# Last block of a three-block network: the order of remainders, residual additions, turns of x and ScalarE's work around the output projection and the query projection

## The reference, cut to what matters

```python
def second_block(x, mem, positions, ...):
    h = rmsnorm_2(x, norm_mix_g)
    x = x + parallel_mixer(h, ...)            # mLSTM heads and causal attention, then @ w_out
    h = rmsnorm_2(x, norm_x_g)
    mem_n = rmsnorm_2(mem, norm_mem_g)
    x = x + memory_cross_attention(h, mem_n, wq_x, wkv_x, xq_norm_g, xk_norm_g, wo_x)
    h = rmsnorm_2(x, norm_ffn_g)
    x = x + jnp.square(jax.nn.relu(h @ w_ff1)) @ w_ff2
    return x

def memory_cross_attention(h, mem_n, wq_x, wkv_x, xq_norm_g, xk_norm_g, wo_x):
    q = rmsnorm_2((h @ wq_x).reshape(Bn, S, 4, 128), xq_norm_g)
    k, v = ...                                # mem_n @ wkv_x, k normed with xk_norm_g
    s = jnp.einsum('bshd,bnhd->bhsn', q, k) * 128 ** -0.5
    o = jnp.einsum('bshn,bnhd->bshd', jax.nn.softmax(s), v)
    return o @ wo_x
```

## Time and profile before

| | |
|---|---|
| three runs | 1669.36, 1673.74, 1679.61 us, median 1673.74 |
| profiled execution | 1671.81 us, span 1670.0 us |
| busy in the span | TensorE 1321.4 us (79%), VectorE 574.6 (34%), ScalarE 369.8 (22%), GpSimd 28.0 (2%) |
| chain that ended last | TensorE 43%, DMA 42%, VectorE 8%, ScalarE 3% |
| granted TensorE clock, mean | 0.908 of full |

### The profile page before, as it was taken

How to read it: one execution, slowest core, us unless ns; L and a number is a source line. 1 busy time by engine, 2 the same in 40 slices (tenths; PEclk the granted TensorE clock), 3 DMA queues, 4 the chain that set the end, 5 groups by cost and what they waited for, 6 DMA issues and landing times.

```text
span 1670.0 us, 30118 instructions
## 1 busy us (share of the span) xinstructions
PE 1321.4 (79%) x12602; PEld 898.3 (54%) x12602; DVE 574.6 (34%) x1202; ACT 369.8 (22%) x642; POOL 28.0 (2%) x54
## 2 busy tenths in 40 slices
PE   4899998765666666789877666666668998889999
PEld 2798584432223223389744322322225887779997
DVE  2575663111001001047531101001013677765555
ACT  2412532000000000054400000000003335544443
POOL 3020100000000000000000000000000000000000
PEclk8999999989888788799999878889788999999999
DMA  9988799999999999995799999999999630455540
GB/s 341 357 279 303 256 403 390 398 422 422 422 422 422 422 421 422 416 361 170 265 420 410 422 422 422 421 422 422 422 422 390 210 130 27 127 177 187 192 151 26
DMA packets 145936, 548.40 MB, mean 328 GB/s; under 512 B 9742, under 2 KB 77744, under 8 KB 96840
## 3 DMA queue, kind: packets, MB, share of 16 engines
q1 hardware_dynamic: 143216, 542.97, 82.9%
q10 hardware_dynamic: 1080, 3.64, 0.6%
q0 software_dynamic: 1568, 0.77, 0.4%
HBM read 546.29 MB, written 1.05 MB: 328 GB/s over the span
## 4 chain that ended last, share of the span: by engine, by line
PE 43%; DMA 42%; DVE 8%; ACT 3%; issue 2%; SPq 1%; DVEq 0%; ACTq 0%
DMA ring<-in_moe_w_up 33%; PE bank L766 8%; DMA ring<-in_moe_w_down 7%; PE bank L880 5%; PE bank L607 5%; PE bank L1302 5%; PE bank L567 3%; PE bank L903 2%; PE bank L630 2%; PE bank L661 2%; DMA ring<-in_attn_w_in 1%; DMA ring<-in_ada_w 1%; DVE ring_split L1620 1%; PE bank L781 1%; SPq L2686 1%
## 5 line engine op out<-in xcount | busy, mean ns | idle before, releaser
L880 PE MATMUL bank<-ring,scratch 128*32 128x256 f32 x3840 | 295.8, 456 | 151.5 <-DMA ring<-in_moe_w_up 102.5
L880 PEld LDWEIGHTS bank<-ring,scratch 128*32 128x32 f32 x3840 | 131.1, 127 | 302.6 <-DMA ring<-in_moe_w_up 158.2
L903 PE MATMUL bank<-ring,scratch 128*32 128x256 f32 x1984 | 153.1, 453 | 60.6 <-DMA ring<-in_moe_w_down 45.5
L1576 DVE COPY scratch<-bank 128x256 f32<-128x256 f32 x32 | 13.6, 425 | 430.0 <-PE bank L889 430.0
L766 PE MATMUL bank<-scratch_split,ring_split 128*128 128x256 f32 x1248 | 151.2, 283 | 3.7 <-DVE ring_split L1620 3.7
L766 PEld LDWEIGHTS bank<-scratch_split,ring_split 128*128 128x128 f32 x1248 | 150.3, 191 | 5.3 <-DVE ring_split L1620 4.1
L903 PEld LDWEIGHTS bank<-ring,scratch 128*32 128x32 f32 x1984 | 64.6, 127 | 142.3 <-DMA ring<-in_moe_w_down 76.4
L1620 DVE TENSOR_TENSOR ring_split<-ring,ring_split 128x2048 fp32r<-128x2048 f32 x48 | 110.0, 2292 | 74.2 <-ACT ring_split L2270 74.0
L2257 ACT ACTIVATE scratch<-bank 128x256 f32<-128x256 f32 x32 | 12.3, 384 | 484.9 <-PE bank L880 484.9
L2270 ACT CAST ring_split<-ring 128x2048 fp32r<-128x2048 f32 x48 | 91.5, 1907 | 59.8 <-PE bank L1302 36.7
L1583 DVE TENSOR_TENSOR scratch<-bank,moe_gate 128x256 f32<-128x256 f32 x32 | 13.6, 425 | 241.0 <-PE bank L903 241.0
(11 more groups left out here) (462 smaller groups left out, 1584.5 us busy)
## 6 DMA issues: line engine op xcount, KB each, us to landing
ring<-in_moe_w_down SPq DMA_DIRECT2D x124, 1024.0 KB, 26.4
ring<-in_moe_w_gate SPq DMA_DIRECT2D x120, 1024.0 KB, 25.1
ring<-in_moe_w_up SPq DMA_DIRECT2D x120, 1024.0 KB, 26.6
ring<-in_ada_w SPq DMA_DIRECT2D x48, 1024.0 KB, 9.2
ring<-in_w_ff SPq DMA_DIRECT2D x32, 1024.0 KB, 5.4
ring<-in_conv_w_in SPq DMA_DIRECT2D x12, 1024.0 KB, 12.4
ring<-in_attn_w_in SPq DMA_DIRECT2D x10, 1024.0 KB, 11.5
ring<-in_w_in SPq DMA_DIRECT2D x7, 1024.0 KB, 12.0
```

The costliest lines, as they stand in the source:

```text
L880: mm = nc.tensor.matmul(GU[32 * j:32 * j + 32, m * 256:(m + 1) * 256], xs[:, k % 2, 16 * k - k % 2 * 16:16 * k - k % 2 * 16 + 32], W[k % 2 ...
L903: mm = nc.tensor.matmul(Y[32 * g:32 * g + 32, 0:256], actT[:, b, 32 * j:32 * j + 32], W[b][:, g * 256:(g + 1) * 256], start=(j + b == 0), ...
```

## The change

On TensorE: the keys are turned ahead of out2.0; n3.3 is turned within qx.0's first pass, behind the first two quarters; the query heads are turned in two goes, each behind the evacuation of its unit, and the scores wait for the second tile only at the fifth; n4.0 to n4.2 go to banks 4 to 6 and n4.3 to bank 7, within ff1.0's first pass behind the first two quarters; the accumulators are claimed at ff2.0 and not ahead of ff1.0. On VectorE: the remainder of ff1.0's weights stands behind the second addition of ox, that of ff1.1's behind the third, and the row remainders behind all four. On ScalarE: in the causal attention the evacuation of out2m.0 and the rounding of out2.0's weights stand behind the last copy of probabilities and not ahead of it; n3.1 and n3.2 are rounded ahead of the last squares; the roots of the query heads and the load of the exponential's table stand between the two tiles of heads.

```diff
@@ -536,9 +536,9 @@
 
             return slice(256 * (k // 2) + k % 2, 256 * (k // 2) + 256, 2)
 
-        def pe_turn_rows(pe, name, src, n=KD, paired=False):
-
-            for b in range(n // 2):
+        def pe_turn_rows(pe, name, src, n=KD, paired=False, tiles=None):
+
+            for b in tiles or range(n // 2):
                 T = tile(pe, f"{name}.{b}")
                 for i in range(4):
                     k, t = 2 * b + i // 2, i % 2
@@ -546,9 +546,9 @@
                     mm = nc.tensor.transpose(T[:, i * P:(i + 1) * P], src[:, t, cols], ident)
                 done(f"{name}.{b}", mm)
 
-        def pe_turn_part(pe, name, u):
-
-            T = tile(pe, f"{name}.{u}")
+        def pe_turn_part(pe, name, u, bank=None):
+
+            T = tile(pe, f"{name}.{u}", bank=bank)
             for i in range(4):
                 k = 2 * u + i // 2
                 mm = nc.tensor.transpose(T[:, i * P:(i + 1) * P], x[:, i % 2, k * P:(k + 1) * P], ident)
@@ -610,7 +610,8 @@
             in0_read[u] = (full[place[name][0]], place[name][1])
             release[seat[("in0", u)]] = in0_read[u]
 
-        def pe_late(pe, n, name, h, rows=None, ts=range(TT), bank=None):
+        def pe_late(pe, n, name, h, rows=None, ts=range(TT), bank=None, last_turn=None):
+
 
 
             key, k0, kk = LATE[n]
@@ -623,6 +624,8 @@
             whole_bank = len(ts) == TT
             for i, (ht, wt) in enumerate(((h[0], hi), (h[0], lo), (h[1], hi))):
                 for k2 in range(0, kk, 2):
+                    if last_turn is not None and i == 0 and k2 == kk // 2:
+                        last_turn()
                     if rows and i != 1:
                         sig(rows[i // 2]).take(pe)
                     for t in ts:
@@ -742,6 +745,9 @@
 
             sig("w_hi").take(pe, (1, len(CONV_ORDER))[p])
             for b in range(4):
+                if p == 1 and b == 2:
+                    sig("x_ready").take(pe)
+                    pe_turn_part(pe, "n4", 3, bank=7)
                 sig(("h1_hi", "h4_hi")[p]).take(pe)
                 run(hi, h[0], (2 * b, 2 * b + 1), first=True)
             pe_split_unit(pe, p, 0)
@@ -1255,27 +1261,33 @@
                 pe_late(pe, u, f"out2m.{u}", (hm_hi, hm_lo))
             sig("oa_ready").take(pe)
             pe_turn_rows(pe, "oaT", oa, 4)
+            sig("kx_ready").take(pe)
+            pe_turn_rows(pe, "kxT", kx, 4)
             for u in range(4):
                 pe_late(pe, 4 + u, f"out2.{u}", (oa_hi, oa_lo), ("oa_hi", "oa_lo") if u == 0 else None)
-                if u == 1:
-                    sig("kx_ready").take(pe)
-                    pe_turn_rows(pe, "kxT", kx, 4)
                 if u >= 1:
                     sig("x_ready").take(pe)
                     pe_turn_part(pe, "n3", u - 1)
-            sig("x_ready").take(pe)
-            pe_turn_part(pe, "n3", 3)
+
+            def turn_last():
+                sig("x_ready").take(pe)
+                pe_turn_part(pe, "n3", 3)
+
+            pe_late(pe, 8, "qx.0", (h3_hi, h3_lo), ("h3_hi", "h3_lo"), last_turn=turn_last)
+            pe_late(pe, 9, "qx.1", (h3_hi, h3_lo))
             for u in range(2):
-                pe_late(pe, 8 + u, f"qx.{u}", (h3_hi, h3_lo), ("h3_hi", "h3_lo") if u == 0 else None)
-            copied(pe, "qx.0")
-            copied(pe, "qx.1")
-            pe_turn_rows(pe, "qxT", qx, 4)
-            for n in ("kxT.0", "kxT.1", "qxT.0", "qxT.1"):
+                copied(pe, f"qx.{u}")
+                pe_turn_rows(pe, "qxT", qx, 4, tiles=(u,))
+            for n in ("kxT.0", "kxT.1", "qxT.0"):
                 copied(pe, n)
-            pe_attend(pe, "c", 8, lambda i: 2,
-                      lambda T, i: nc.tensor.matmul(T[:, 0:SEQ], qxT[:, i // 2, (i % 2) * P:(i % 2 + 1) * P],
-                                                    kxT[:, i // 2, :], start=True, stop=True),
-                      lambda i, b: vx[:, b, (i // 2) * P:(i // 2 + 1) * P])
+
+            def score_c(T, i):
+                if i == 4:
+                    copied(pe, "qxT.1")
+                return nc.tensor.matmul(T[:, 0:SEQ], qxT[:, i // 2, (i % 2) * P:(i % 2 + 1) * P],
+                                        kxT[:, i // 2, :], start=True, stop=True)
+
+            pe_attend(pe, "c", 8, lambda i: 2, score_c, lambda i, b: vx[:, b, (i // 2) * P:(i // 2 + 1) * P])
             for i in range(8):
                 copied(pe, f"co{i}")
             pe_turn_rows(pe, "oxT", ox, 4)
@@ -1283,14 +1295,13 @@
                 pe_late(pe, 10 + u, f"ox.{u}", (ox_hi, ox_lo), ("ox_hi", "ox_lo") if u == 0 else None)
                 if u >= 1:
                     sig("x_ready").take(pe)
-                    pe_turn_part(pe, "n4", u - 1)
-            sig("x_ready").take(pe)
-            pe_turn_part(pe, "n4", 3)
-            acc = [tile(pe, f"ff2.{i}", bank=4 + i) for i in range(4)]
+                    pe_turn_part(pe, "n4", u - 1, bank=3 + u)
             for n, (name, u) in enumerate(FF_ORDER):
                 if name == "ff1":
                     pe_turned_split(pe, 1, n, f"ff1.{u}", (h_hi, h_lo), bank=u % 4)
                 else:
+                    if u == 0:
+                        acc = [tile(pe, f"ff2.{i}", bank=4 + i) for i in range(4)]
                     sig("w_split").take(pe)
                     release[seat[(name, u)]] = (sig("w_split").sem, sig("w_split").taken[pe.engine])
                     hi, lo = (z[n % 2].rearrange("p (a n) -> p a n", a=2) for z in w_parts[1])
@@ -2129,14 +2140,9 @@
                     empty(v, f"n4.{b}", ins)
                     give("h4_split", V.tensor_copy(st[:, 249:250], ident[:, 0:1]))
 
-            rest_of_weights(1, 0)
-
-            def beside_ox():
-                rest_of_weights(1, 1)
-                rest_of_rows((0, 1))
-
-            residual("ox", 4, None, "x_ready", beside=beside_ox)
-            rest_of_rows((2, 3))
+            residual("ox", 4, None, "x_ready", between=lambda: rest_of_weights(1, 0),
+                     beside=lambda: rest_of_weights(1, 1))
+            rest_of_rows(range(4))
             sig("squares_ready").take(v)
             step(V.tensor_reduce(rs4, pieces[:, :, 0:4], AX, ALU.add))
             step(V.tensor_scalar(rs4, rs4, 1.0 / D, EPS, ALU.mult, ALU.add))
@@ -2557,7 +2563,7 @@
                             load_table(ACT.Exp)
                         if i == 6:
                             round_late(8)
-                        if i == 7:
+                        if i == 8:
                             part_out("out2m", 0, part2)
                             round_late(4)
 
@@ -2575,17 +2581,19 @@
             load_table(ACT.Sqrt)
             for i in range(4):
                 if i >= 2:
-                    rounded("n3", "h3_hi", h3_hi, plain("norm_x_g_2"), (i - 2,))
+                    rounded("n3", "h3_hi", h3_hi, plain("norm_x_g_2"), (0,) if i == 2 else (1, 2))
                 sig("x_ready").take(s)
                 ins = piece_squares((i,), 256)
             sig("squares_ready").give(ins)
-            rounded("n3", "h3_hi", h3_hi, plain("norm_x_g_2"), (2, 3))
+            rounded("n3", "h3_hi", h3_hi, plain("norm_x_g_2"), (3,))
             round_late(9)
             roots(rs3, 2)
             round_late(10)
             round_late(11)
-            turned("qxT", qxT, lambda k: (vcol("xq_norm_g_2"), None), (0, 1))
+            turned("qxT", qxT, lambda k: (vcol("xq_norm_g_2"), None), (0,))
             roots(qn, 8)
+            load_table(ACT.Exp)
+            turned("qxT", qxT, lambda k: (vcol("xq_norm_g_2"), None), (1,))
             attend("c")
             round_late(12)
             for b in range(2):
```

## The result

| | before | after |
|---|---|---|
| 20 runs each, median | 1673.62 us (1665.34 to 1679.61) | 1665.20 us (1657.71 to 1671.21) |
| profiled execution, span | 1670.0 us | 1663.4 us |

The ratio is 0.995 with a 95% interval of 0.9937 to 0.9963: the change takes 6 to 10.5 us off, 8.4 in the medians, where 7.3 were forecast. Both programs scatter by some 14 us from run to run, so the interval is wide beside the effect, and what the single steps did is read from the traces.

What follows compares the result with a forecast made beforehand. TensorE was taken as the bound of the feed-forward loop; 6.1 us at the output projection and ff1.0 plus 1.2 upstream made 7.3, so 1671.8 became 1664.5, or 1666.5 us as a median, range 1660.5 to 1673.5.

Steps and rivals of the forecast that it cites:

- The bound and the place of the gain: TensorE bounds the feed-forward loop from 1492.61 us, so moving ff1.0's end moves the kernel's end one for one.
- Output projection and ff1.0: From ox.0 to ff1.0's end: VectorE's additions go first, TensorE's waits shrink, ff1.0 ends at 1486.5 us, gaining 6.1 us.
- The 1.6 us for the spell: In ff1.0: the half-clock stretch behind TensorE's 3 us of idleness goes away, 7.24 less 5.65 us.
- Rival (a): In ff1.0: part still runs at 1.2 GHz, gain 5.7 us, 1668.0 us; chance 0.17.
- they add no wait: Turns of x in banks 4 to 7: each is emptied by the addition giving x_ready, so no wait is added.
- Upstream: Query projection and query heads, ahead of ox: gain 1.2 us, with bounds of -0.3 and +2.8.
- The turns' 0.6: Out2 and query projection: earlier keys' turns and n3.3 within qx.0 let qx.1 end at 1444.1 us, gaining 0.6.
- first exponential at 1449.1: 1.2 us earlier: ScalarE in the cross attention: two head copies precede the root, so the exponential starts 1.2 us sooner, 0.6 included.
- The load's own price: ScalarE ahead of the first exponential: one table load as before, costing 1.28 us and no more.
- I leave the spell where it is: Cross attention: despite some 3 us of new TensorE idle time, the half-clock stretch at 1448 to 1452 us stays unchanged.
- Ahead of out2.0: End of the first attention: ScalarE's order starts its last product about 1 us earlier, but gains nothing towards oaT's rounded rows.
- Loop: Feed-forward loop to the end: it stays unchanged and only starts earlier.

Runs made afterwards that it cites:

- before_again: The unchanged kernel before, profiled once more on another chip: ox.0 to ff1.1 took 25.5 us, the loop's ff1 unit 5.47 us; no timed ratio.
- up_only: Kernel before plus all of the diff except the parts around ox and ff1.0: ratio 0.9976 to before.
- pe_only: Kernel before plus only TensorE's edits around ox and ff1.0, with VectorE's old order: ratio 0.9994 to before.
- dve_only: Kernel before plus only VectorE's new order around ox, with the old banks and n4.3 ahead of ff1.0: ratio 0.9979 to before.
- acc_late: Kernel before with one line moved, the four accumulators claimed at ff2.0 and not ahead of ff1.0: ratio 1.0002 to before.
- heads_only: Kernel before plus only the query heads turned and copied in two goes, with the exponential's table load between: ratio 0.9998 to before.
- turns_only: Kernel before plus earlier keys' turns, n3.3 within qx.0 and ScalarE's changed order, heads in one go: ratio 0.9999 to before.
- after_again: The changed kernel, unaltered, profiled and timed once more: ratio 0.9955 to before.
- out_only: Kernel before plus only the output projection's part (VectorE's order, banks of n4, n4.3 within ff1.0): ratio 0.9943 to before.
- rows_later: Changed kernel plus two unread VectorE operations, some 2.5 us, ahead of the four row remainders: ox.0 to ff1.1 took 21.4 us, against 19.3.
- fill_c: Changed kernel plus 7 unread products on TensorE ahead of the cross attention's first turn: ratio 0.9941 to before.
- fill_bc: Changed kernel plus unread TensorE products, 4 ahead of the causal attention's sixth turn and 7 ahead of the cross attention's first: ratio 0.9919 to before.

## Why the prediction was right, and where a step was not

**The bound and the place of the gain** stood as put: the loop begins earlier, and the end with it.

**Output projection and ff1.0:** 6.1 forecast, 6.24 in the pair of profiles, and 5.9 to 6.3 in the table (25.4 to 25.6 less 19.3 to 19.5), where ff1.0 had half clock before. Counted from ox.0, the end of ff1.0 is within 0.3 us of the working (19.3 against 19.6), partly by luck: ff1.0 began 0.6 us earlier than forecast (12.4 against 13.0) and took 6.9 us until ff1.1's first product against 6.6. The times between are within 0.5. The 1.6 us for the spell, though, are not gained every time. Of the eight profiles in which TensorE or VectorE keeps an order of before there, four had it (before, before_again, up_only, pe_only) and four had not (dve_only, acc_late, heads_only, turns_only). With all of the order of before, B is 25.4 to 25.6 with the spell and 23.8 without. So the part is worth 6.2 us against a run with the spell and 4.4 against one without, and the forecast of 6.1 assumed a run with it. The rule of the Trainium skill that the prediction weighed (TensorE: Matmul & The Clock Gate, Part 1), that a spell's place changes from run to run, is borne out for the order of before: the same wait of 3 us was followed by half clock in before and not in acc_late, which differs by one claim. Rival (a), the spell staying in the changed order, was seen in none of the six profiles with this part (after, after_again, out_only, rows_later, fill_c, fill_bc).

**Banks:** "they add no wait" held, but their worth was missed: without them VectorE's order costs 2.07 us of wait again (dve_only).

**Upstream:** 1.2 forecast and 1.21 measured, by half for the wrong reason, so that the agreement is luck. The turns' 0.6 is confirmed by turns_only; with full clock in the cross attention the whole upstream part is worth 0.7 (A is 47.0 in out_only, and 46.2 to 46.3 in rows_later, fill_c and fill_bc). The step that failed is "first exponential at 1449.1: 1.2 us earlier": the new time was right and the old one to compare it with was not, since 1450.29 holds a wait that half clock made. The load's own price was read rightly: in the changed kernel the next copy starts 0.13 us behind its end (1450.62 + 1.28 = 1451.90, then 1452.03). The Trainium skill's 2.66 us for a switch (ScalarE: Activation LUTs, What ACT_TABLE_LOAD costs) isn't borne out here either. What the pair of profiles shows in its place is some 0.6 us (1.21 less 0.65) from another position of the spell. The new idle time was taken as neutral ("I leave the spell where it is"); a spell followed it in four of the five profiles that have the new heads' order with nothing filled in (not in rows_later), shorter than the one before, at some 1.3 us each (A 47.5 against 46.2).

**Ahead of out2.0** the prediction took ScalarE's new order at nothing. That holds where the causal attention has a short spell or none, and not where it has a long one. Counted from the last block's first product of 384 columns, out2.0 starts 84.1 us later in seven profiles, three of them with the old order (before, dve_only, pe_only) and four with the new (turns_only, rows_later, fill_c, fill_bc). In the other seven the spell there was about twice as long as in before. The old order then took 85.6 to 86.0 us (before_again, heads_only, acc_late, out_only), the new one 84.5 to 84.8 (after, after_again, up_only). TensorE in order of time, before_again:

```profile
...
1407.32 3.78 PE L630 MATMUL bank<-ring_split,hT_split 128*128 128x256 f32 x16
...
1414.85 0.71 PE L708 MATMUL bank<-scratch 128*128 128x128 f32 x4 [1.43 <-ACT scratch L2549]
...
1425.69 2.27 PE L630 MATMUL bank<-ring_split,hT_split 128*128 128x256 f32 x16 [0.76 <-ACT hT_split L2464]
...
```

The same places in the changed kernel:

```profile
...
1404.83 3.78 PE L633 MATMUL bank<-ring_split,hT_split 128*128 128x256 f32 x16
...
1411.27 0.71 PE L711 MATMUL bank<-scratch 128*128 128x128 f32 x4 [0.28 <-ACT scratch L2555]
...
```

In both, out2m.0's first pass runs at half clock, and what follows comes late. In the new order ScalarE makes the last copy of probabilities ahead of out2m.0's evacuation and of the rounding, 73.6 us behind the same first product and not 74.7, and TensorE waits 0.28 us for it and not 1.43. With a short spell the copy comes sooner too, but out2.0 doesn't: there something else holds it. So the part ahead of out2.0 is worth some 1 us in executions with a long spell. No run has this edit alone.

**Loop:** "unchanged" held for the program. The 2.9 us between the two profiles are a matter of the execution; before_again has the short spacing too.

**Median:** 1666.5 forecast, 1665.2 measured. Turns 0.6, output 4.4 to 6.2 and the shorter spell in the cross attention make 5 to 7.5 us, and the causal attention adds up to 1 in executions with a long spell there. The timed interval of 6.2 to 10.5 allows that, so a median within 1.3 us of the forecast is closer than the sum could promise. Whether the loop's shorter spacing is commoner in one program can't be told from one profile each.

## What to carry to other kernels

When a busy engine waits for another's queue, look in that queue for work whose taker comes later than the waiter's, and put it behind; then look which PSUM bank the next claim needs, since a moved evacuation moves the bank's release with it, and either edit alone may bring half or nothing. Before a row's duration is taken as the price of an order, look at the granted clock there, or an edit is credited with what the clock did. Filling a gap of some microseconds on TensorE that can't be closed with products that nobody reads is worth a trial: here both profiles so filled had no spell behind the gap in the cross attention, and the timed runs lean the same way without settling it.

## What the runs showed of the hardware that was not expected

The same program ran its ff1 units at two rates at a granted clock of 1.00: products 118 ns apart from start to start (5.65 us for 48) or 114 ns (5.47). Each execution kept one of the two from its second unit to its last, 14 units, and changed it, if at all, between the first and the second (after, before_again: 5.65, then 5.47). Of 14 profiles, 4 had the longer spacing in the loop. What decides is open; it is worth 2.9 us here.

Whether idleness of 1.1 to 3.3 us on TensorE was followed by half clock went by place, but not surely. The gap of some 2 us in the causal attention was followed by it in all 13 profiles that left it open, the gaps in the cross attention in 10 of 12 (not in rows_later, after 3.3 us, nor in out_only), those of 2.1 to 3.0 us before or in ff1.0 in 4 of 8, and the one of 1.1 to 1.9 us before n4.0 in none of 7. With the gap in the cross attention filled there was none in either profile made (fill_c, fill_bc).
